# A transformer block on one core: a new order of jobs in the up-projection, and VectorE's small operations of differential attention as steps of their own

## The chip, the cores and the metric
The kernel runs on one core of one Trainium2 chip. The metric is device time in microseconds, the median of 3 runs. "Faster" and "slower" are against the kernel before.

## The reference, cut to what matters
One block over 2048 tokens and 16 meta tokens in front of them, float32 throughout. Two groups of heads run on the same input. The first is differential attention with ALiBi:

```
s1 = q1 k1^T * scale + bias ;  s2 = q2 k2^T * scale + bias      (per head, 4 heads)
a  = softmax(s1) - lam * softmax(s2) ;  o = a v
```

The second is latent attention (4 heads), whose queries are `_rms(cq) @ w_q_up` with a rotary part. Both outputs go through `w_o`, an RMSNorm and the residual; a squared-ReLU MLP of width 4096 follows. The mask lets a query see the chunks of 64 keys up to its own, so row tile i of 128 queries reads 16 + 128 (i + 1) keys.

## The kernel before, in words
The stages run one after the other: projections, `up-projection` of the latent queries, differential attention, latent attention, output product, MLP. A stage is a program for each engine, written in order; the engines meet only through semaphores that count up. Where an operation needs float32 accuracy from PE's fast format, an operand is split: ScalarE rounds it to a high half, VectorE subtracts to get the low half, and PE adds three products.

**Up-projection (line 797).** A list `jobs` (lines 838 to 840) sets the order on all engines at once. A job is a `turn` (four transposes of a weight), a `fold` (query weights times key weights), a `rope` half (rotary queries of a piece of 512 tokens), a `q` (the other queries of a head) or a `vo` (values' weights times w_o). PE writes the job's sums into the next of 8 banks and waits until the job 8 banks back has been taken. `takers` gives who takes them: VectorE rotates ropes (two multiplications each, GpSimd adds them), and copies of `q` and `vo` go to ScalarE and VectorE in turn. Results go to one of 8 output slots, `slot(engine, i)`: the slot is free once the store that used it 8 results before has landed. SP issues the stores in the order of the jobs, and at the first half of rope pieces 2 and 3 loads for the next stage in front of them. At the same two places, `WO_AT` (line 840), ScalarE makes the high half of a part of w_o (2 of 4 heads), VectorE the low half, and the `vo` products behind it wait for that (`wo_lo_ready`). At the second of them ScalarE first loads the table for exponentials.

**Differential attention (from line 1167).** For each of 4 heads, row tiles i = 0 to 15 with two components c. A row is cut in chunks of at most 512 keys (`row_chunks`). For a chunk PE makes scores in one of 4 banks; VectorE adds the bias, writes the row and keeps a maximum (L1535, a second instruction reads the accumulator); behind a row's last chunk it reduces the maxima to minus the row's maximum (L1542). ScalarE takes the exponential over the whole row with its sum (L1481). For component 0 VectorE takes the reciprocal of the sum (L1567) and GpSimd scales the row (L1473). For component 1 VectorE takes the reciprocal (L1574), multiplies by minus lambda (L1576), and adds both components (L1580): "the sum of row tile i" below. When the four row tiles of a group are summed, PE transposes them tile by tile (L1646), ScalarE copies (L1494) and PE multiplies by the values (L1660).

`head_steps` writes one order of steps for all engines: `chunk`, `exp`, `scale`, `end`, and between them `turn`, `product` and `out`, spread over three phases of a head (row tiles 0 to 7, 8 to 11, 12 to 15) by a cost of each step of VectorE. The first phase holds the turns of the last group of the head before, the second those of groups 0 and 1, the third those of group 2. The first turn of a group isn't put in front of its last `end`. `SCALE_AFTER` and `END_AFTER` say how many chunks later a row's scaling and sum come. Each engine walks the same list and does the steps that are its own.

## Time and profile before
| | us |
|---|---|
| median of 3 runs | 2596.75 (2596.61 to 2596.9) |
| profiled execution | 2593.93, its span 2592.2 |
| up-projection | about 391.9 to 426.6 |
| differential attention | about 426.6 to 796 |
| PE busy, share of the span | 2531.8, 98% |
| VectorE | 1613.4, 62% |
| ScalarE | 1212.7, 47% |
| GpSimd | 333.4, 13% |

Times in the rows are microseconds from the span's start. A busy engine can still be late: "idle before" names what ended the time in which it had nothing to run, and a matmul's duration is its latency, while the next one starts before it ends.

### The profile page before, as it was taken

What the parts mean: (1) busy time and instruction counts of PE and PEld (TensorE: products, weight loads), DVE (VectorE), ACT (ScalarE), POOL (GpSimd) and SP (SyncE); (2) the same over time, 40 slices, a digit from 0 to 9 for tenths busy, and PEclk for the clock granted to TensorE, in tenths of its full rate; (3) what the DMA queues carried; (4) which work ended last, traced back from release to release, by engine and by line L of the source; (5) the groups of instructions that cost most, each with busy time, mean ns of one, the idle gap of its engine ahead of it and who ended that gap; (6) DMA issues with size and microseconds to landing.
All of it is one profiled execution on the core that took longest, in us unless ns stands there. A gap on an engine that the chain in (4) does not pass through costs nothing.

```text
span 2592.2 us, 35303 instructions
## 1 busy us (share of the span) xinstructions
PE 2531.8 (98%) x12172; PEld 2107.2 (81%) x12172; DVE 1613.4 (62%) x3499; ACT 1212.7 (47%) x2183; POOL 333.4 (13%) x368
## 2 busy tenths in 40 slices
PE   8999999999999999989999999999999999999997
PEld 8998887676667999978877888888888888888886
DVE  6123307998985776654468777867758465564765
ACT  6112314777765555554544333533335353443544
POOL 2110002222211222210000000000000001121143
PEclk9999999999999999999999999999999999999999
DMA  7334458554342111145677666666655365776787
GB/s 236 119 106 125 123 163 261 136 135 99 82 140 85 34 29 46 42 130 161 194 240 223 210 219 215 219 193 209 190 163 175 118 216 106 179 161 164 200 162 136
DMA packets 328892, 398.33 MB, mean 154 GB/s; under 512 B 20864, under 2 KB 235120, under 8 KB 320400
## 3 DMA queue, kind: packets, MB, share of 16 engines
q1 hardware_dynamic: 311152, 364.15, 44.6%
q0 software_dynamic: 17568, 31.99, 8.5%
q8 instruction: 95, 1.56, 0.2%
q14 instruction: 77, 0.63, 0.1%
HBM read 239.60 MB, written 156.48 MB: 153 GB/s over the span
## 4 chain that ended last, share of the span: by engine, by line
PE 62%; DVE 3%; DMA 1%; ACT 1%; issue 1%; SPq 0%; POOL 0%; DVEq 0%; ACTq 0%; POOLq 0%
PE ff_ps_x L3266 26%; PE ff_ps_m L3266 13%; PE ff_ps_z L3266 6%; PE ml_ps_s L2143 6%; PE ff_ps_m L1699 4%; PE ml_ps_o L2172 4%; PE ml_ps_t L2156 2%; DMA ml_v_raw<-scr_yT 1%; DMA ff_pieces<-scr_acc 0%; PE ff_ps_r L2703 0%; PE mo_ps_t L2720 0%; SPq L2330 0%; DVE ff_pieces L2433 0%; DVE ff_pieces L2624 0%; DVE ff_pieces L2620 0%
## 5 line engine op out<-in xcount | busy, mean ns | idle before, releaser
L3266 PE MATMUL ff_ps_x<-ff_mv_hi_p,ff_st_hi_p 128*128 128x512 f32 x764 | 297.8, 390 | 0.5 <-ACT ff_u L3006 0.5
L3266 PE MATMUL ff_ps_x<-ff_mv_hi_p,ff_st_lo_p 128*128 128x512 f32 x764 | 297.3, 389 | 0.0
L3266 PE MATMUL ff_ps_x<-ff_mv_lo_p,ff_st_hi_p 128*128 128x512 f32 x764 | 297.2, 389 | 0.0
L2143 PE MATMUL ml_ps_s<-wide,ml_qs 128*128 128x416 f32 (+14 forms) x880 | 194.4, 353 | 4.1 <-PEq L137 2.8
L3112 DVE TENSOR_TENSOR ff_st_lo_p<-ff_ps_m,ff_st_hi_p 128x512 fp32r<-128x512 f32 x190 | 130.5, 687 | 103.4 <-ACT ff_st_hi_p L2989 103.4
L2956 POOL DMA_DIRECT2D scr_acc<-ff_pieces x64 | 55.6, 874 | 1015.2 <-DVE ff_pieces L3136 946.7
L3006 ACT ACTIVATE ff_u<-ff_ps_x 128x512 f32<-128x512 f32 x128 | 76.6, 598 | 214.8 <-PE ff_ps_x L3266 214.8
L3266 PEld LDWEIGHTS ff_ps_x<-ff_mv_hi_p,ff_st_hi_p 128*128 128x128 f32 x764 | 143.4, 188 | 32.5 <-issue 2.0
L3266 PEld LDWEIGHTS ff_ps_x<-ff_mv_hi_p,ff_st_lo_p 128*128 128x128 f32 x764 | 143.4, 188 | 30.0
L3266 PEld LDWEIGHTS ff_ps_x<-ff_mv_lo_p,ff_st_hi_p 128*128 128x128 f32 x764 | 143.4, 188 | 29.5
L2143 PEld LDWEIGHTS ml_ps_s<-wide,ml_qs 128*128 128x128 f32 x880 | 150.4, 188 | 17.0 <-issue 2.9
L2989 ACT ACTIVATE ff_st_hi_p<-st_raw 128x512 fp32r<-128x512 f32 x191 | 119.4, 626 | 86.2 <-PE ff_ps_z L3266 86.2
L3266 PE MATMUL ff_ps_m<-wide,ff_st_hi_p 128*128 128x512 f32 x512 | 157.7, 389 | 0.4 <-DVE ff_st_lo_p L2607 0.4
L2989 ACT ACTIVATE ff_st_hi_p<-ff_ps_m 128x512 fp32r<-128x512 f32 x190 | 113.2, 598 | 93.6 <-PE ff_ps_m L3266 93.6
L3266 PE MATMUL ff_ps_x<-wide,ff_st_hi_p 128*128 128x512 f32 x504 | 155.1, 389 | 0.0
L3112 DVE TENSOR_TENSOR ff_st_lo_p<-st_raw,ff_st_hi_p 128x512 fp32r<-128x512 f32 x191 | 130.8, 687 | 36.9 <-ACT ff_st_hi_p L2989 35.6
L2058 DVE CUSTOM_DVE_ANT_0 ml_rows<-ml_ps_s,ahead_bias 128x416 f32<-128x416 f32 (+14 forms) x176 | 100.1, 570 | 70.4 <-PE ml_ps_s L2143 62.6
L1660 PE MATMUL da_ps_o<-da_pT,da_v 128*128 128x512 f32 (+3 forms) x320 | 137.2, 529 | 0.0
L1981 ACT ACTIVATE ml_pT_hi<-ml_ps_t 128x512 fp32r<-128x512 f32 (+3 forms) x176 | 90.8, 538 | 93.3 <-PE ml_ps_t L2156 92.9
L2080 DVE TENSOR_TENSOR ml_pT_lo<-ml_ps_t,ml_pT_hi 128x512 fp32r<-128x512 f32 (+3 forms) x176 | 105.2, 615 | 41.6 <-ACT ml_pT_hi L1981 41.3
L1613 PE MATMUL da_ps_s<-da_keys,ahead_q 128*128 128x416 f32 (+14 forms) x352 | 112.5, 423 | 2.4 <-DVE da_mx L1535 2.4
L3266 PEld LDWEIGHTS ff_ps_m<-wide,ff_st_hi_p 128*128 128x128 f32 x512 | 96.0, 188 | 20.5 <-issue 0.6
(318 smaller groups left out, 6329.4 us busy)
## 6 DMA issues: line engine op xcount, KB each, us to landing
st_raw<-in_w_ff SPq DMA_DIRECT2D x64, 512.0 KB, 6.4
scr_hid<-ff_pieces SPq DMA_DIRECT2D x128, 256.0 KB, 2.7
st_raw<-scr_hid SPq DMA_DIRECT2D x64, 512.0 KB, 5.3
ring<-in_w_ff SPq DMA_DIRECT2D x28, 1024.0 KB, 7.5
scr_t<-ring SPq DMA_DIRECT2D x24, 1024.0 KB, 5.6
ring<-scr_t SPq DMA_DIRECT2D x21, 1024.0 KB, 7.6
scr_acc<-ff_pieces POOLq DMA_DIRECT2D x64, 256.0 KB, 4.0
ring<-scr_u SPq DMA_DIRECT2D x13, 1024.0 KB, 8.0
```

The costliest lines, as they stand in the source:

```text
L1613: m = pe.matmul(ps_s[n % NSB][:, 0:w], qs[:, g % 2, c, P * b:P * b + P], keys[u][:, 2 * c + j, k0:k0 + w], start=j == 0, stop=j == 1)
L1660: pe.matmul(ps_o[:, c0:512], v_meta[:, :] if t == 0 else v[:, t - 1], pT[0:rows_of, n % NPT, c0:512], start=t == 0, stop=t == tiles_of(g) ...
L1699: m = pe.matmul(bank, y[a][:, k], w[b][:, cols], start=k == 0 and i == 0, stop=k == KD - 1 and i == 2, skip_group_check=True)
L1981: act.activation(pT_hi[0:rows_of, n % NPT, c0:512], ps_t[n % NTB][0:rows_of, c0:512], ACT.Copy).then_inc(hi_copied, 1)
L2058: dve.tensor_tensor_reduce(out=row(i, u)[:, k0:k0 + w], in0=ps_s[n % NSB][:, 0:w], in1=bias[:, b0:b0 + w], scale=1.0, scalar=LOWEST, op0=A ...
L2080: dve.tensor_tensor(pT_lo[0:rows_of, n % NPT, c0:512], ps_t[n % NTB][0:rows_of, c0:512], f32(pT_hi[0:rows_of, n % NPT, c0:512]), ALU.subtr ...
L2143: m = pe.matmul(ps_s[n % NSB][:, 0:w], q, k, start=j == 0, stop=j == len(pairs) - 1)
L2172: m = pe.matmul(ps_o[:, c0:512], v[0:rows_of, at_v], p, start=t == 0 and j == 0, stop=t == tiles_of(g) - 1 and j == 2)
L2989: act.activation(st_hi[kind][:, :, :], stationary(kind, n % 2), ACT.Copy).then_inc(st_hi_ready, 1)
L3006: act.activation(tile, bank[:, :], ACT.Copy).then_inc(taken, 1)
L3112: dve.tensor_tensor(st_lo[kind][:, :, :], stationary(kind, n % 2), f32(st_hi[kind][:, :, :]), ALU.subtract).then_inc(st_lo_ready, 1)
L3266: m = pe.matmul(bank[:, :], w[kind][:, k], a[kind][:, k], start=start and k == 0 and i == 0, stop=stop and k == KH - 1 and i == 2, skip_gr ...
```

## The change
In the up-projection the list of jobs has a new order. In differential attention the small operations of VectorE become steps of their own, a chunk or more behind what they read: `most` (the row's maximum), `invert` and `weigh` (the two in front of the sum). A row's sum comes a few chunks after its second component ends, counted by the next row's chunks, and in front of its successor's scaling. The small tiles have four slots in place of two; the second components of row tiles 0 to 2 lie beside one another. A cost in the planner goes from 250 to 100.

```
-        jobs += [("q", 0, h) for h in range(MLA_H)] + [("turn", TURN_V)] + ropes_of(2) + folds_of((0, 1)) + ropes_of(3) + folds_of((2, 3))
+        jobs += ropes_of(2) + [("turn", TURN_V)] + [("q", 0, h) for h in range(2)] + folds_of((0, 1))
+        jobs += [("q", 0, h) for h in range(2, MLA_H)] + ropes_of(3) + folds_of((2, 3))
...
         def comp_row(i, c, u):
-            return row(i, u) if c == 0 else second[:, i % 2, 0:META + P * (i + 1)]
+            if c == 0:
+                return row(i, u)
+            start, wide = (sum(META + P * (a + 1) for a in range(i)), 0) if i < 3 else (0, i % 2)
+            return second[:, wide, start:start + META + P * (i + 1)]
...
-                        steps += [step for _, step in later if step[2] - NT * step[1] < i]
-                        later = [(left, step) for left, step in later if step[2] - NT * step[1] >= i]
-                        later.append((1, ("exp", 0, i, c)))
+                        due = i if c == COMPS - 1 else i - 1
+                        if i < 3:
+                            due = -1
+                        steps += [step for _, step in later if step[2] - NT * step[1] < due]
+                        later = [(left, step) for left, step in later if step[2] - NT * step[1] >= due]
+                        later += [(1, ("most", 0, i, c)), (1, ("exp", 0, i, c))]
                         if c == 0:
                             later.append((SCALE_AFTER, ("scale", 0, i)))
                         if c == COMPS - 1:
-                            later.append((END_AFTER, ("end", 0, i)))
+                            later += [(after, (kind, 0, i)) for kind, after in zip(("invert", "weigh", "end"), end_after(i))]
...
+        def end_after(i):
+            first = {NT - 1: 5, 0: 3, 1: 3, 2: 3}.get(i) or len(row_chunks(i + 1)) + 1
+            return first, first + 1, first + 2
...
-            return META + P * (step[2] + 1) + 250 if step[0] == "end" else 0
+            return META + P * (step[2] + 1) + 100 if step[0] == "end" else 0
...
-        SCALE_AFTER, END_AFTER = 2, 5
+        SCALE_AFTER = 3
...
+                if c == 1 and k0 == 0 and not (first_head and i < 4):
+                    dve.wait_ge(probs_ready, NT * h + (-1 if i < 3 else 0 if i == 3 else i - 1))
...
-                if k0 + w == META + P * (i + 1):
-                    dve.wait_ge(scores_read, NCH * h + n + 1)
-                    dve.tensor_scalar(nmax_all[:, 0:nth + 1], mx[:, i % 2, c, 0:nth + 1], -scale, None, ALU.mult, ALU.min,
-                                      accum_out=nmax[:, i % 2, c:c + 1]).then_inc(max_ready, 1)
...
+            def most(h, i, c, **at):
+                last = max(n for n, chunk in enumerate(chunks) if chunk[:2] == (i, c))
+                parts = len(row_chunks(i))
+                dve.wait_ge(scores_read, NCH * h + last + 1)
+                dve.tensor_scalar(mx[:, i % 4, c, 0:parts], mx[:, i % 4, c, 0:parts], -scale, None, ALU.mult, ALU.min,
+                                  accum_out=nmax[:, i % 4, c:c + 1]).then_inc(max_ready, 1)
...
-            heads(dve, {"chunk": chunk, "scale": invert, "end": end})
+            heads(dve, {"chunk": chunk, "most": most, "scale": invert_first, "invert": invert_second, "weigh": weigh_second, "end": end})
```

`invert_first`, `invert_second` and `weigh_second` hold the three small operations of before, each behind its own wait; `end` keeps the addition.

## Rows read from the trace of the kernel before
**Rows 1.** Stretches: length; busy of PE, PEld, DVE, ACT, POOL; PE clock, DMA, GB/s
```profile
402.40:426.60 24.20, 18.94 (x78) 14.88 (x77) 15.87 (x20) 9.19 (x10) 7.75 (x7) 0.93 1.04 323
426.60:454.00 27.40, 27.05 (x135) 23.16 (x134) 24.62 (x124) 18.74 (x44) 5.84 (x8) 1.00 0.76 240
454.00:512.30 58.30, 54.85 (x270) 40.26 (x269) 55.00 (x194) 42.24 (x65) 13.28 (x9) 1.00 0.65 150
512.30:598.80 86.50, 83.50 (x417) 61.43 (x417) 78.46 (x305) 63.17 (x112) 19.08 (x16) 1.00 0.45 111
```
**Rows 2.** Timeline, end of head 1: start, us, engine, line, operation [idle <-releaser]
```profile
591.51 0.63 PE L1613 MATMUL da_ps_s<-da_keys,ahead_q 128*128 128x400 f32 x2 [0.75 <-DVE da_mx L1535]
592.37 3.43 PE L1660 MATMUL da_ps_o<-da_pT,da_v 128*128 128x512 f32 x8
598.79 1.09 PE L1646 MATMUL da_ps_t<-ident,da_rows 128*128 128x128 f32 x8 [1.25 <-DVE da_rows L1580]
...
593.78 2.02 ACT L1481 ACTIVATE da_second<-da_second,da_nmax 128x2064 f32<-128x2064 f32 x1 [2.64 <-DVE da_nmax_all L1542]
...
595.92 0.17 DVE L1574 RECIPROCAL da_inv<-da_total 128x1 f32<-128x1 f32 x1 [1.61 <-ACT da_second L1481]
```
**Rows 3.** Timeline of PE, for the pace of scores and of transposes
```profile
585.79 1.09 PE L1613 MATMUL da_ps_s<-da_keys,ahead_q 128*128 128x416 f32 x5
...
642.54 0.60 PE L1646 MATMUL da_ps_t<-ident,da_rows 128*128 128x128 f32 x4
```
**Rows 4.** Timeline of PE in the up-projection
```profile
413.35 0.47 PE L989 MATMUL mu_ps<-mu_wo_hi,mu_turned_hi 128*128 128x512 f32 x1 [2.15 <-DVE mu_wo_lo L962]
...
422.18 0.47 PE L989 MATMUL mu_ps<-mu_wo_hi,mu_turned_hi 128*128 128x512 f32 x1 [3.12 <-DVE mu_wo_lo L962]
...
424.09 0.63 PE L989 MATMUL mu_ps<-mu_wo_hi,mu_turned_hi 128*128 128x512 f32 x1
```
**Rows 5.** Timeline of the up-projection on VectorE, GpSimd and ScalarE
```profile
402.64 2.48 DVE L975 TENSOR_TENSOR mu_rot<-mu_ps,up_trig 128x512 f32<-128x512 f32 x4 [1.42 <-issue]
410.91 2.29 DVE L962 TENSOR_TENSOR mu_wo_lo<-mu_wo_first,mu_wo_hi 128x2048 fp32r<-128x2048 f32 x1 [1.11 <-ACT mu_wo_hi L946]
...
404.01 2.55 POOL L933 TENSOR_TENSOR mu_out<-mu_rot 128x512 f32<-128x512 f32 x2 [2.54 <-DVE mu_rot L975]
...
415.89 0.60 ACT L953 ACTIVATE mu_out<-mu_ps 128x512 f32<-128x512 f32 x1 [0.92 <-DMA scr_mq<-mu_out]
```
**Rows 6.** DMA issues (last: us to landing); below, the eight stores until 410.9
```profile
scr_w_vo<-mu_out SPq DMA_DIRECT2D x8, 256.0 KB, 4.9
mu_wo_first<-in_w_o SPq DMA_DIRECT2D x1, 1024.0 KB, 5.0
...
L925 SPq DMA_DIRECT2D scr_mq<-mu_out x4: 467/1071/1327, 407.0 to 410.0; - x4
DMA to landing us min/median/max: 7.6/8.3/10.6
```
**Rows 7.** Timeline of VectorE in head 2, row tiles 11 to 13
```profile
655.88 0.16 DVE L1567 RECIPROCAL da_inv<-da_total 128x1 f32<-128x1 f32 x1
655.95 0.60 DVE L1535 CUSTOM_DVE_ANT_0 da_second<-da_ps_s,ahead_bias 128x448 f32<-128x448 f32 x1
...
656.91 0.09 DVE L1535 DVE_READ_ACCUMULATOR2_ANT da_mx<- 128x1 f32 x1
657.03 0.16 DVE L1542 TENSOR_SCALAR_CACHE_REDUCE da_nmax_all<-da_mx 128x4 f32<-128x4 f32 x1
...
657.15 0.66 DVE L1535 CUSTOM_DVE_ANT_0 da_rows<-da_ps_s,ahead_bias 128x480 f32<-128x480 f32 x1
...
659.55 0.16 DVE L1574 RECIPROCAL da_inv<-da_total 128x1 f32<-128x1 f32 x1
659.74 0.21 DVE L1576 TENSOR_SCALAR da_inv<-da_inv,da_lam 128x1 f32<-128x1 f32 x1
659.99 1.97 DVE L1580 SCALAR_TENSOR_TENSOR da_rows<-da_second,da_inv,da_rows 128x1680 f32<-128x1680 f32 x1
```

More of the change, by code:

```diff
@@ L1559, in minus_lambda, with invert_first @@
                 dve.wait_ge(lam_step, 4)
-            def invert(h, i, u, **at):
+            def invert_first(h, i, u, **at):
                 dve.wait_ge(exp_ready, NT * COMPS * h + COMPS * i + 1)
-                if not (isinstance(h, int) and h == 0 and i < 2):
-                    dve.wait_ge(first_scaled, NT * h + i - 1)
-                dve.reciprocal(inv[:, i % 2, 0:1], total[:, i % 2, 0:1]).then_inc(inv_ready, 1)
-            def end(h, i, u, **at):
+                if not (isinstance(h, int) and h == 0 and i < 4):
+                    dve.wait_ge(first_scaled, NT * h + i - 3)
+                dve.reciprocal(inv[:, i % 4, 0:1], total[:, i % 4, 0:1]).then_inc(inv_ready, 1)
@@ L1575, in end @@
-                dve.wait_ge(inv2_step, n + 1)
-                dve.tensor_scalar(inv2[:, i % 2:i % 2 + 1], inv[:, i % 2, 1:2], lam[:, 3:4], None, ALU.mult).then_inc(inv2_step, 1)
-                dve.wait_ge(inv2_step, n + 2)
+                dve.wait_ge(second_inverted, NT * h + i + 1)
+                dve.tensor_scalar(inv2[:, i % 4:i % 4 + 1], inv[:, i % 4, 1:2], lam[:, 3:4], None, ALU.mult).then_inc(second_weighed, 1)
+            def end(h, i, u, **at):
+                dve.wait_ge(second_weighed, NT * h + i + 1)
@@ L1578, in end @@
                 dve.wait_ge(first_scaled, NT * h + i + 1)
-                dve.scalar_tensor_tensor(out=row(i, u), in0=comp_row(i, 1, u), scalar=inv2[:, i % 2:i % 2 + 1], in1=row(i, u),
+                dve.scalar_tensor_tensor(out=row(i, u), in0=comp_row(i, 1, u), scalar=inv2[:, i % 4:i % 4 + 1], in1=row(i, u),
                                          op0=ALU.mult, op1=ALU.add).then_inc(probs_ready, 1)
-            heads(dve, {"chunk": chunk, "scale": invert, "end": end})
+            heads(dve, {"chunk": chunk, "most": most, "scale": invert_first, "invert": invert_second, "weigh": weigh_second, "end": end})
```

28 lines of the change are left out of this document (14 added, 14 removed).

## The prediction
> **What bounds the kernel now.** I read the page first: PE is busy 98% of the span and VectorE 62%, but the change touches only 390 to 796 us, so the share of the span says little. The table of stretches [rows 1] is the next thing: from 402.4 to 426.6 us (the up-projection after its first jobs) PE is busy 18.9 of 24.2 us at a mean granted clock of 0.93; in differential attention PE and VectorE are both nearly full, 83.5 and 78.5 of 86.5 us for each head in the middle. A head lasts 86.5 us: the stretches are cut where PE waits for the sum of row tile 15 [rows 1, 2].
>
> Which of the two it is that ends a wait in attention, the waits of PE show: 0.75 us behind VectorE's reads at the end of a head, 1.25 us for the sum of row tile 15 (the first transposes of the last group) [rows 2]. Read from start to start, where one matmul should follow the other at its own pace, these and the small ones come to about 4.3 us a head. The rest, about 82 us, is PE's own work. I check that: 8 product matmuls take 3.43 us from first start to last end, so 0.43 us each; 4 transposes take 0.60 us with 0.27 us of that the last one's, so 0.11 each; score matmuls of 416 columns come every 0.185 us (5 in 1.09 us, the last one 0.35) [rows 2, 3]. A head has 88 product matmuls with 38,912 columns (32.6 us), 152 transposes (16.7 us) and 176 score matmuls with 70,656 columns (31.4 us): 80.7 us, and a little for the changes between kinds. So VectorE can save at most 4.3 us a head before PE is the bound.
>
> **Part 1, the new order of jobs.** In the order of before PE waits twice for the low half of w_o, 2.15 and 3.12 us. Soon behind the second wait a matmul takes 0.63 us in place of 0.47 [rows 4]: the granted clock is at the lower level, 1.2 in place of 2.4 GHz, after those 3.1 us without work. A mean of 0.93 over 24.2 us [rows 1] makes that 1.7 us lost. Behind the first wait of 2.15 us the matmuls stay short.
>
> First wait, after: PE starts rope piece 2 at 402.4 us, in place of the queries, and has 12 matmuls of 512 columns for it (0.23 us each at the score rate of [rows 3], 2.7 us), 0.4 us for the turn of v and 2.7 for two queries: it is at its first fold at 408.2 us. VectorE's queue in front of that fold: rotations of piece 1 from 402.64 us (2.48), low half of w_o (2.29), rotations of piece 2 (2.48), low half of the turned v (the size of a rotation's quarter, 0.7 us) [rows 5]. That is 410.6 us, so PE waits 2.4 us. The first part of w_o landed 5.0 us after its issue [rows 6], before any of this, so nothing waits for it. Two queries (2.7 us) are then still to do, which were done at 413.35 us before: the two orders are level. No gain.
>
> Second wait, after: PE is through with rope piece 3 at 418.9 us, as before. What it waits for is a chain: ScalarE's copy of query 2, load of its table, high half of w_o, VectorE's low half. Before, the copy in front of the table load began at 415.89 us, itself released by a store that had landed [rows 5], and PE went on at 422.18: 6.29 us from copy to PE. In the new order the sums of query 2 are there at 414.9 us; if the copy began then, PE would go on 1 us earlier, and might keep its clock: 1.0 + 1.7 = 2.7 us gained. But query 2 now has output slot 4 (of 8, the 13th store), which rope (2,0) has used, and must wait until that has landed. VectorE rotates piece 2 only from 407.4 us; GpSimd's addition starts 1.37 us after a rotation starts (402.64 to 404.01) and takes 1.28, so the store is issued at 410.1 us. By then SP has issued as many bytes as before (three 256 KB query stores then, 0.78 MB of queries and bias now, which its place in front of rope piece 2 brings forward), and the store issued at 410.0 us landed after 7.6 us [rows 6]. So the copy starts at 417.6 us in place of 415.89: +1.7 us. The ends of this cost: -2.7 us (lands at once; the later stores of the folds took 4.9 us in the median, which would be -0.9) and +4.5 us (the slowest store's 10.6 us) [rows 6]. I take +1.7; the lower clock is lost either way. VectorE's copy of query 3 waits for the next slot until 418.6 us, in the cover of ScalarE's table load and high half. On SP the keys of the third group are issued behind the same four folds as before, near 420 us, and are read only near 454 us.
>
> What follows is PE-bound until 454 us (27.05 of 27.4 us [rows 1]), so the 1.7 us reach the end.
>
> **Part 2, what VectorE saves.** A small operation that depends on the one before it: the accumulator's read starts at 656.91 us, the reduction behind it at 657.03, its own read at 657.11, the next read of scores at 657.15: 0.24 us. One that depends on nothing recent: read of the accumulator and reciprocal both at 655.88, the next scores at 655.95, 0.07 us [rows 7]. So each of 128 maxima gains 0.16 us behind the next chunk (0.12 of wait, 0.04 of start). Of the pair in front of a sum, reciprocal 659.55, product 659.74, sum 659.99: 0.44 us, of which two independent steps would leave 0.08 + 0.12 (the product's 0.21 is longer than the reciprocal's 0.16): 0.24 gained for each of 64 sums. Together 20 + 15 = 35 us of VectorE's time over four heads, 9 a head. To it comes the wait for ScalarE's last exponential of a head, 1.61 us [rows 2], under which now lie reads of the next head. The new wait in front of the second component's first chunk asks for a sum two row tiles back: nothing. Between no gain of VectorE at all (the durations of [rows 7] in any place) and 35 us I take 35; the row of the reciprocal is the same kind of operation in the same place.
>
> The Trainium skill speaks against this. "VectorE: DVE Perf Modes", in the section "The DRAIN you can't avoid", says that the next operation starts only when the pipeline is empty, that the semaphore costs nothing, and advises to save operations, not waits. By that rule the 35 us would be near 0, and the result that of the last rival below; these rows do not agree, since the held reduction starts 0.12 us later than the free reciprocal does.
>
> **Part 3, what becomes of it.** VectorE's 9 us a head are more than PE's 4.3 us of waits, so PE decides, and its waits for sums move. I wrote out both orders of steps.
> - Row tile 11's sum, which PE needs for the first transpose of the third group, came right behind the first component of row tile 12, three chunks of scores before that transpose in every head. Now it stands behind the third of four chunks of the second component, and PE's queue has only the last two, narrow products of the group before (256 and 128 columns twice, 0.65 us) between that chunk and the transpose. VectorE needs 0.54 for the chunk (448 columns at 1.04 ns and 0.08 to start, the pace of the sums) and 1.83 for the sum (the 1.97 of row tile 12's, less 128 columns) [rows 7]: PE waits 2.37 - 0.65 = 1.7 us, in all four heads. New.
> - Row tile 15's sum: from the start of the head's last chunk VectorE has, at that pace, 0.49 for it, 0.23 for the next head's first, 0.16 until the maximum is there; from the start of ScalarE's exponential to the reciprocal are 2.14 us (593.78 to 595.92); in its cover the next four chunks; then the reciprocal, one more chunk (0.5), small steps (0.4), another chunk (0.38), the sum (1.97 and three times 128 columns, 2.37, less 0.08 of overlap): 7.0 us. PE has 5.8 us of work from there to its transpose (six products 3.9, seven chunks 1.9) and is 0.7 us ahead, because VectorE has just done row tile 14's sum: 2.0 us of wait, where 0.75 + 1.25 us and a wait for ScalarE's first copy stand now [rows 2].
> - What goes besides these: the small waits for reads.
> So a head in the middle has about 3.8 us of waits in place of 4.3: 0.5 us gained, 1.5 over three. In head 0, which has no products of a head before it, VectorE is the bound from 454 us on (55.0 of 58.3 us busy [rows 1]): there 8 row tiles give 0.56 us each, 4.5 us, less 1.7 of the new wait and what PE allows: 2.3 us. The tail behind the last scores is as long as before, since no chunk is left to lie in front. Scaling by GpSimd, busy 19 of 86.5 us, starts a chunk later and in front of nothing that waits.
>
> **The sum.** +1.7 - 1.5 - 2.3 = -2.1 us. Against the profiled execution (span 2592.2, with what lies around it 2593.93 us) that is 2591.8; against the median, 2.8 us higher, 2594.6.
>
> **Rivals.** A measurement of this kernel tells 0.2% (5.2 us) from no change.
> - *PE's waits mostly go.* If VectorE's lead is large enough at both sums, only one wait of 1.3 us a head is left of 4.3: 3 us gained a head, 12 in all, 2586.5 with part 1. For it: 9 us of VectorE's time a head. Against it: at the sum of row tile 11 PE's queue is empty by the order itself, whatever VectorE's lead.
> - *The store lands in time.* Part 1 gains 2.7 in place of losing 1.7: 2590.2. For it: fewer small stores in front. Against it: none of the eight issued before 411 us landed within 7.5 us [rows 6].
> - *Slower: VectorE is behind at the two sums.* Each chunk that it lags there (0.54 us) is added to PE's wait, at 4 + 3 places: 3.8 us a chunk. PE can be up to 4 chunks ahead, the number of score banks. From two chunks of lag on it is slower than before (2602), at three 2606. For it: between the two sums VectorE has some 22 us of work in PE's 21. Against it: PE has just held more work than VectorE in front of row tile 11's sum.
> - *The small operations cost as much between reads as behind them.* Then VectorE saves nothing, the stretch from row tile 11's sum to that of 15 takes 31.3 in place of 29 us, a head 0.8 us more than now: 2600.5.
>
> **How the numbers follow.** Forecast 45% (its own range 2591 to 2598.5), waits go 22%, store in time 12%, VectorE behind 13%, no saving 8%. The range reaches into the first and the slower rival: 2586 to 2603. Faster by over 0.2%: 22 + 10 + 5 = 37%; slower 11 + 3 + 1 = 15%; same 48%.
>
> **What would show it.** PE waiting some 1.7 us for the sum at the first transpose of the third group in each head, and some 2 us at row tile 15's, with no wait for reads at a head's end beyond 0.3 us; maxima and reciprocals on VectorE with no idle time in front; heads of 86 us; in the up-projection ScalarE's copy of query 2 released by a store, and a second wait of PE near 5 us. The prediction is wrong if a head is under 84.5 or over 87.5 us, or if that copy starts before 416 us.

## The result and the profile after

The changed kernel takes 2612.42 us in the median (2611.51 to 2612.98), the kernel before 2596.72 us beside it: the ratio is 1.0064, 95% interval 1.0052 to 1.0076. Forecast were 2594.6 us in a range to 2603. The change makes the kernel slower, and both halves of it do (the experiments below).

The profiled executions differ by 19.0 us of span (2611.2 against 2592.2). By the starts of the stages and heads in the two timelines that is: attention starts 3.4 us later, head 0 is 0.5 us longer, heads 1 and 2 are 5.1 and 4.8 us longer (91.4 us each), the last head with the tail 4.0, and 1.3 us come later. By the prediction's own sign (a head over 87.5 us) it is wrong.

First the stretches that answer to [rows 1], of after (columns as there); the third and fourth are cut, as before, where PE waits for row tile 15's sum.

```profile
402.40:430.00 27.60, 20.25 (x80) 15.92 (x79) 15.94 (x20) 7.59 (x10) 9.80 (x7) 0.89 0.99 315
430.00:457.40 27.40, 27.40 (x137) 23.82 (x135) 22.00 (x121) 18.22 (x44) 5.12 (x7) 0.99 0.65 202
457.40:518.90 61.50, 54.70 (x271) 40.92 (x270) 56.16 (x220) 44.99 (x74) 14.98 (x11) 1.00 0.61 147
518.90:610.40 91.50, 85.84 (x417) 64.52 (x417) 75.09 (x305) 63.53 (x112) 19.21 (x16) 0.96 0.43 105
```

VectorE is busy 75.1 us where it was 78.5, so its work did get less. PE is busy 85.8 where it was 83.5, with the same 417 matmuls, at a clock of 0.96 where it was 1.00: its work didn't grow, it was done more slowly. And PE is idle 5.7 us of the head where it was idle 3.0.

The up-projection, timeline of after on PE, ScalarE and VectorE (start, us, engine, line, operation, idle before and its releaser), against [rows 4, 5]:

```profile
411.17 0.47 PE L990 MATMUL mu_ps<-mu_wo_hi,mu_turned_hi 128*128 128x512 f32 x1 [2.24 <-DVE mu_turned_lo L967]
...
424.71 0.77 PE L990 MATMUL mu_ps<-mu_wo_hi,mu_turned_hi 128*128 128x512 f32 x1 [5.11 <-DVE mu_wo_lo L963]
...
418.41 0.60 ACT L954 ACTIVATE mu_out<-mu_ps 128x512 f32<-128x512 f32 x1 [2.71 <-DMA scr_mqr<-mu_out]
419.03 1.28 ACT L945 ACT_TABLE_LOAD   x1
420.32 1.91 ACT L947 ACTIVATE mu_wo_hi<-mu_wo_second 128x2048 fp32r<-128x2048 f32 x1
...
419.50 0.69 DVE L982 COPY mu_out<-mu_ps 128x512 f32<-128x512 f32 x1 [3.48 <-DMA scr_mqr<-mu_out]
422.27 2.29 DVE L963 TENSOR_TENSOR mu_wo_lo<-mu_wo_second,mu_wo_hi 128x2048 fp32r<-128x2048 f32 x1 [2.08 <-ACT mu_wo_hi L947]
```

PE waits 2.24 and 5.11 us, where it waited 2.15 and 3.12. The second wait is the chain forecast: a copy of a query waits for a store, behind it in ScalarE's queue stand the table load and the high half of w_o, and VectorE's low half ends the wait. The first matmul behind it takes 0.77 us, so the clock is down. The stretch at the lower clock (after) is:

```profile
424.00:430.80 6.80, 6.09 (x17) 4.96 (x17) 4.17 (x7) 1.19 (x2) 2.66 (x3) 0.50 0.93 271
```

PE is busy for 6.1 of its 6.8 us, the first 0.7 us still belong to the wait. So it costs 3.0 us, where the 3.4 us of the kernel before cost 1.7.

VectorE's small operations, timeline of after, against [rows 7]:

```profile
687.06 0.08 DVE L1549 DVE_READ_ACCUMULATOR2_ANT da_mx<- 128x1 f32 x1
687.06 0.15 DVE L1561 TENSOR_SCALAR_CACHE_REDUCE da_mx<-da_mx 128x4 f32<-128x4 f32 x1
687.14 0.08 DVE L1561 DVE_READ_ACCUMULATOR da_mx<-da_mx 128x1 f32 x1
687.14 0.59 DVE L1549 CUSTOM_DVE_ANT_0 da_rows<-da_ps_s,ahead_bias 128x416 f32<-128x416 f32 x1
...
690.33 0.21 DVE L1594 TENSOR_SCALAR da_inv<-da_inv,da_lam 128x1 f32<-128x1 f32 x1
690.45 0.58 DVE L1549 CUSTOM_DVE_ANT_0 da_second<-da_ps_s,ahead_bias 128x416 f32<-128x416 f32 x1
```

The reduction starts with the accumulator's read and the next scores start 0.08 us later; the product costs 0.12. In the kernel before the same reduction kept VectorE for 0.24 us. At this place the forecast holds to the hundredth. Its total doesn't show: 9 us of VectorE's time a head were forecast, its busy time fell by 3.4, and all of its gaps under 0.15 us came to no more than 2.3 us a head before.

PE in the same head, timeline of after, around its three waits:

```profile
610.37 1.59 PE L1666 MATMUL da_ps_t<-ident,da_rows 128*128 128x128 f32 x12 [2.34 <-DVE da_rows L1600]
...
614.38 0.96 PE L1666 MATMUL da_ps_t<-ident,da_rows 128*128 128x128 f32 x4
...
668.56 0.66 PE L1666 MATMUL da_ps_t<-ident,da_rows 128*128 128x128 f32 x4 [1.93 <-DVE da_rows L1600]
...
672.31 1.01 PE L1666 MATMUL da_ps_t<-ident,da_rows 128*128 128x128 f32 x4
...
693.81 0.52 PE L1633 MATMUL da_ps_s<-da_keys,ahead_q 128*128 128x272 f32 x2 [1.10 <-DVE da_mx L1549]
```

PE waits 2.34 us for row tile 15's sum (1.25 in [rows 2]), 1.93 for row tile 11's (a new wait), and at the head's end it still waits 1.10 for reads. And a group of 4 transposes takes 0.96 and 1.01 us behind the first two waits, where [rows 3] has 0.60. The same head cut at the clock (stretches of after; the clock is third from the end):

```profile
602.75:611.70 8.95, 6.61 (x35) 4.67 (x33) 6.74 (x39) 5.81 (x15) 2.12 (x3) 1.00 0.30 83
611.70:615.10 3.40, 3.40 (x13) 2.35 (x11) 1.47 (x8) 1.59 (x5) 0.77 (x1) 0.50 0.02 5
615.10:669.70 54.60, 52.43 (x264) 39.17 (x263) 44.67 (x185) 38.43 (x70) 11.16 (x10) 1.00 0.61 146
669.70:673.10 3.40, 3.40 (x15) 2.88 (x13) 2.34 (x9) 2.30 (x4) 0.72 (x1) 0.50 0.91 218
673.10:694.20 21.10, 20.00 (x103) 15.29 (x102) 20.07 (x71) 15.24 (x23) 4.45 (x3) 1.00 0.03 4
```

Two stretches of 3.4 us at 1.2 GHz, each just behind a wait, and each with PE busy throughout. Read in this way over the whole of attention, after has six such stretches, before has one, in the tail:

```profile
771.20:774.60 3.40, 2.90 (x13) 2.90 (x14) 3.27 (x7) 1.20 (x2) 0.00 (x0) 0.51 0.00 0
```

Of after's seven new or longer waits for sums, idle 1.93 us (row tile 11) and 2.34 us (row tile 15), five have such a stretch behind them: head 0's at row tile 11 and head 2's at row tile 15 have none. The sixth stretch is in the tail, behind 3.33 us. A PE that is full does half as much in 3.4 us, so one stretch costs 1.7 us.

### The profile page after: what moved, and what is told of

The parts are those of the page before. It is cut to its first block, busy times and chain, and to the rows that moved or that the text cites. A ratio compares the mean times of both kernels' runs of the same rounds, so it can differ in the third digit from the quotient of the medians.

```text
span 2611.2 us, 35301 instructions
## 1 busy us (share of the span) xinstructions
PE 2537.2 (97%) x12172; PEld 2116.0 (81%) x12172; DVE 1599.0 (61%) x3499; ACT 1212.5 (46%) x2183; POOL 335.8 (13%) x368
## 4 chain that ended last, share of the span: by engine, by line
PE 62%; DVE 3%; DMA 1%; ACT 1%; issue 1%; SPq 0%; POOL 0%; DVEq 0%; ACTq 0%; POOLq 0%
PE ff_ps_x L3286 26%; PE ff_ps_m L3286 13%; PE ff_ps_z L3286 6%; PE ml_ps_s L2163 6%; PE ff_ps_m L1719 4%; PE ml_ps_o L2192 4%; PE ml_ps_t L2176 2%; DMA ml_v_raw<-scr_yT 1%; DMA ff_pieces<-scr_acc 0%; PE ff_ps_r L2723 0%; PE mo_ps_t L2740 0%; SPq L2350 0%; DVE ff_pieces L2453 0%; DVE ff_pieces L2644 0%; DVE ff_pieces L2640 0%
## 5 line engine op out<-in xcount | busy, mean ns | idle before, releaser
L2001 ACT ACTIVATE ml_pT_hi<-ml_ps_t 128x512 fp32r<-128x512 f32 (+3 forms) x176 | 90.7, 538 | 93.4 <-PE ml_ps_t L2176 91.6
L1666 PE MATMUL da_ps_t<-ident,da_rows 128*128 128x128 f32 x608 | 96.9, 283 | 18.1 <-DVE da_rows L1600 18.1
```

Source lines behind the costliest of these rows:

```text
L1666: m = pe.transpose(ps_t[n % NTB][0:rows_of, P * b:P * b + P], row(4 * g + b, u)[:, k0:k0 + rows_of], ident[:, :])
L2001: act.activation(pT_hi[0:rows_of, n % NPT, c0:512], ps_t[n % NTB][0:rows_of, c0:512], ACT.Copy).then_inc(hi_copied, 1)
```

## The experiments

All times are medians; "ratio" is against the kernel before, run on the same chip beside them.

**Each half alone.** The kernel before with the new order of jobs, and the changed kernel with the old order:

```
-        jobs += [("q", 0, h) for h in range(MLA_H)] + [("turn", TURN_V)] + ropes_of(2) + folds_of((0, 1)) + ropes_of(3) + folds_of((2, 3))
+        jobs += ropes_of(2) + [("turn", TURN_V)] + [("q", 0, h) for h in range(2)] + folds_of((0, 1))
+        jobs += [("q", 0, h) for h in range(2, MLA_H)] + ropes_of(3) + folds_of((2, 3))
```

> The kernel before with the new order of jobs alone. Theory: after's trace has PE wait 5.11 us at its second wait for the low half of w_o in place of 3.12, since ScalarE's copy of query 2 stood 2.71 us until a store of a rope had landed, and the granted clock is at the lower level for 6.8 us from 423.9 us on in place of 3.4; differential attention begins 3.4 us later in after, and that is what this order costs: 2600 us, heads of attention at 86.5 us. Rival: the order costs nothing by itself, and the start is late for another reason (the stage before it ended 0.45 us later): 2597.

> The changed kernel with the old order of jobs. Theory: the rest of the loss lies in attention, where after's heads last 91.4 us in place of 86.5 and PE waits 2.1 us for row tile 11's sum and 2.5 us for row tile 15's; 2596.7 + 12 to 14 = 2609 to 2611 us. Rival: a good part of attention's loss comes from its late start and the loads that collide with it, then heads are shorter here than 91 us and the time is under 2606.

Measured: the order alone 2600.46 us against 2596.65, ratio 1.0013 (1.0003 to 1.0022); the steps alone 2607.76, ratio 1.0043 (1.0028 to 1.0058). The order alone is where its expectation had it, the steps alone 1.2 us below theirs. The two losses together, some 0.56%, are the whole change's 0.64% within their intervals: two faults that add up, the larger in attention.

**The sums sooner.** If PE waits because the sums come two chunks later, put them back to the chunk they had:

```
-            first = {NT - 1: 5, 0: 3, 1: 3, 2: 3}.get(i) or len(row_chunks(i + 1)) + 1
-            return first, first + 1, first + 2
+            return (5, 5, 5) if i == NT - 1 else (3, 4, 5)
```

> As the one before (old jobs, small operations as steps), but a row's two small operations and its sum come 3, 4 and 5 chunks behind its second component in every row (5, 5, 5 for row tile 15), so that row tile 11's sum is again one chunk into the second component of row tile 12. Theory (the place of the sums, and not the separate small operations, makes PE wait, and each wait of over 2 us has a stretch at the lower clock behind it, 1.7 us): no wait at the first transpose of the third group, about 1.3 us at row tile 15's, no lower clock between 450 and 760 us, heads of 84 us: 2586 to 2591 us. Rival (the separate small operations themselves delay ScalarE's exponentials and PE): heads stay above 88 us, 2603 or more.

Measured 2627.32 us, ratio 1.0119 (1.0102 to 1.0136): a miss, 20 us slower than the steps alone. Timeline of this kernel, VectorE and ScalarE at row tiles 12 and 13:

```profile
677.25 1.96 DVE L1598 SCALAR_TENSOR_TENSOR da_rows<-da_second,da_inv,da_rows 128x1680 f32<-128x1680 f32 x1
679.13 0.15 DVE L1559 TENSOR_SCALAR_CACHE_REDUCE da_mx<-da_mx 128x4 f32<-128x4 f32 x1
...
679.33 1.81 ACT L1490 ACTIVATE da_rows<-da_rows,da_nmax 128x1808 f32<-128x1808 f32 x1 [2.42 <-DVE da_mx L1559]
...
681.25 0.16 DVE L1582 RECIPROCAL da_inv<-da_total 128x1 f32<-128x1 f32 x1 [0.81 <-ACT da_rows L1490]
```

The maximum is a step one chunk behind its row, and that is the chunk at which the earlier sum falls. The sum, 1.96 us, stands in front of it; the exponential starts that much later (ScalarE waited 2.42 us for the maximum); and two chunks on VectorE itself stands idle 0.81 us for the exponential's total. Moved as steps, the maximum and the sum compete for one place. The changed kernel avoids this by its later sums: that is what their lateness is for, and its price is PE's waits.

**The maximum alone as a step.** Reciprocal, product and sum of the second component together 5 chunks behind the row, the first reciprocal 2 chunks behind, as before the change (the planner's cost and the rule for overdue steps are those of before, too; they aren't shown below):

```
+            return 5, 5, 5
...
+        SCALE_AFTER = 2
```

> Old jobs; of the small operations only the reduction of the maxima is a step of its own, a chunk behind; reciprocal, product and sum stand together 5 chunks behind the row as before, with the planner's old cost and the old rule for what is flushed. Theory: VectorE gains 0.16 us for each of 128 maxima, the waits for sums stay as before, 1.3 us at row tile 15's: heads of 85 us, 2591 to 2594 us. Rival (a later maximum delays the exponential, and with it the copies that PE needs): 2598 or more.

Measured 2663.1 us, ratio 1.0255 (1.0238 to 1.0273), against 2591 to 2594 expected: the worst of all. Waits in one head of this kernel (us in total, times, longest):

```profile
ACT da_rows L1488 <- DVE da_mx L1557: 27.3, 16, 3.2
DVE da_inv L1580 <- ACT da_rows L1488: 14.2, 16, 1.7
DVE da_inv L1584 <- ACT da_second L1488: 8.2, 14, 2.2
```

The same view of the kernel before has 1.2 us, once, in place of the first row, and 0.8 and 1.6 us, once each, in place of the others. Maximum, exponential, reciprocal is a ring between two engines that wait in order. With a chunk added in front of the exponential and none in front of the reciprocal, VectorE waits once for every row, and each wait delays the next maximum. How much of the 66 us this ring costs isn't shown: a sum stands ahead of a maximum here as in sums_early (the sum starts at 658.27, the maximum behind it at 659.79), and attention has some 41 us at the lower clock, up to 20 us of the loss. Neither was tried apart.

**What PE's waits and the clock are worth.** Two edits on the steps alone. One puts both groups' transposes later in the list, the other leaves them and gives PE something to do in the wait (the wait for the bank that the unread transposes write moves in front of them, which isn't shown below):

```
-        PHASES = (((0, 1), ((1, 3),), 0.2, 7), ((2,), ((0, 0), (0, 1)), 0.15, 7), ((3,), ((0, 2),), 0.2, 7))
+        PHASES = (((0, 1), ((1, 3),), 0.4, 7), ((2,), ((0, 0), (0, 1)), 0.15, 7), ((3,), ((0, 2),), 0.3, 7))
...
+                    if g >= 2:
+                        for k in range(12):
+                            pe.transpose(ps_t[n % NTB][:, 0:P], ident[:, :], ident[:, :])
                     pe.wait_ge(probs_ready, NT * h + 4 * g + 4)
```

> Differential attention as in the changed kernel, the old order of jobs in the up-projection, and the transposes of the last group (after row tile 15's sum) and of the third group (after row tile 11's sum) placed about four chunks of scores later in the list. The kernel with the same steps and the transposes at their old places took 2607.8 us. Theory A (the whole loss of attention is TensorE waiting at these two places for a sum that now comes two chunks later, 2.5 + 2.1 us a head, and its lower clock behind the wait, 1.7 us each): both waits fall under 0.5 us, the clock stays up, the heads go back to about 86.5 us from 91.4, and the time is 2590 to 2598 us. Theory B (VectorE's order itself costs it, the exponential and the second sum's place among the reads): waits of the same size come up elsewhere, heads stay at 90 to 91 us, 2604 to 2610 us.

> Differential attention as in the changed kernel, the old order of jobs; ahead of the wait for row tile 11's and for row tile 15's sum TensorE makes 12 transposes of the identity that nobody reads, so that it works through most of a wait that is there anyway. Without them the kernel took 2607.8 us. Theory A (a good half of the loss is the granted clock, which falls behind these waits): the low stretches in attention go away, 6 of them by 1.7 us is 10 us, and the time is 2597 to 2601 us with the waits themselves nearly unchanged in total. Theory B (the clock follows something else, or the time at the lower clock is hidden by VectorE's work): 2606 to 2610 us. If the 12 transposes are longer than the waits, each head becomes up to 0.5 us longer.

Later transposes: 2601.38 us, ratio 1.0029 (1.0019 to 1.004). Kept busy: 2600.79, ratio 1.0024 (1.0014 to 1.0033). By the ratios they win back 3.6 and 5 of the 11 us; the first lies between the ranges of its two theories. PE at the last group's first transpose, first in the kernel kept busy, then in the one with later transposes (timelines):

```profile
603.74 0.71 PE L1662 MATMUL da_ps_t<-ident 128*128 128x128 f32 x5
605.49 1.53 PE L1668 MATMUL da_ps_t<-ident,da_rows 128*128 128x128 f32 x12 [1.03 <-DVE da_rows L1599]
```

```profile
602.45 0.54 PE L1632 MATMUL da_ps_s<-wide,ahead_q 128*128 128x304 f32 x2 [1.73 <-DVE da_mx L1548]
607.16 1.13 PE L1679 MATMUL da_ps_o<-da_pT,da_v_meta 128*128 128x512 f32 x2 [1.92 <-ACT da_pT L1504]
```

With the unread transposes PE still arrives at the sum too early (1.03 us idle instead of 2.34), no sum comes sooner, and yet heads 1 and 2 are 88.2 and 88.3 us instead of 89.8 and 91.6: the granted clock is 1.00 from 429 to 779 us, where the steps alone have three low stretches, one in head 1 and two in head 2. That is what the clock alone cost there. Moving the last group's transposes removes its wait, but in the place of one wait of 2.3 us come two, for VectorE's reads (1.73) and for ScalarE's copies (1.92): turns pushed into a shorter stretch meet their copies late. Theory B was right for this group. (The clock stayed up behind these waits, in all three heads.)

**The maximum in front of the early sum**, and **the second reciprocal and its product alone**, in two versions (the three edits in this order; the last version also has the second reciprocal 3 instead of 2 chunks behind, and the planner's cost back at 250):

```
-                    steps += [step for left, step in later if left <= 0]
+                    steps += sorted((step for left, step in later if left <= 0), key=lambda step: step[0] not in ("most", "exp"))
...
                         steps += [step for _, step in later if step[2] - NT * step[1] < due]
                         later = [(left, step) for left, step in later if step[2] - NT * step[1] >= due]
+                        steps.append(("most", 0, i, c))
...
                     steps += [("chunk", 0, n)]
+                    if k0 + w == META + P * (i + 1):
+                        steps.append(("most", 0, i, c))
```

> Differential attention as in the changed kernel with the old order of jobs, but the sum early (5 chunks behind its row, as before the change) and, where a row's maximum and another row's sum fall on the same chunk, the maximum in front. With the sum in front of the maximum the same places took 2627.3 us. Theory A (that loss was the exponential, which started a sum of 2 us late): the waits of ScalarE for the maximum and of VectorE for the exponential's total go away, transposes of row tiles 11 and 15 don't wait over 1 us, and the time is 2590 to 2600 us. Theory B (the maximum a chunk later is too late whatever stands around it): VectorE still waits for ScalarE, 2610 to 2625 us.

> The kernel before with one part of the change: the second reciprocal and its product with lambda as steps of their own ahead of the sum (2 and 3 chunks behind the row), four slots of the small tiles; the maximum right behind its last read, exponential, first reciprocal, scaling and sum at the places of before. Theory A (VectorE's small operations are worth time where nothing is displaced): VectorE saves 0.1 to 0.24 us at each of 64 sums, 7 to 15 us of its work; what PE waits for sums at the transposes and heads' ends (some 2 us a head before) becomes less: 2590 to 2595 us. Theory B (VectorE has idle time in the heads anyway): no change, 2596 to 2597.5 us. In neither is it slower than 2600 us unless the second reciprocal comes before the exponential is done.

> The kernel before with one part of the change: second reciprocal and its product as steps of their own, where they fit ahead of the sum (3 and 4 chunks behind the row); maximum right behind its last read and ahead of any sum, and all other steps at the places of before. The version of it in which the maximum came behind a sum of another row took 2638 us. Theory A (that loss was the maximum standing behind a sum of 2 us, so that the exponential and then VectorE itself started late): ScalarE's waits for the maximum are back at 11 to 12 us in 90, heads at 86 to 87 us, 2592 to 2598 us. Theory B (VectorE's waits for the exponential's total, 7.7 + 7.7 us in a head, come from the new small steps themselves): heads stay over 89 us, 2605 to 2640 us. On the worth of the small operations: if VectorE's work bounds the head, some 0.1 us at 30 sums is 3 us less in attention; if not, no change against 2596.

With the maximum in front, the early sums take 2612.52 us, ratio 1.007 (1.0053 to 1.0087): 0.49% less, 13 us, than with the sum in front, and still 0.27% more than with the change's own places. The two kernels differ in nothing but this order. ScalarE's wait for the maximum of first components falls from 17.1 to 10.2 us in a head, VectorE's waits for a total from 8.6 to 4.8: the time lies in theory B's range, though theory A's waits did become shorter. The version called max_at_once was meant to have the maximum of before, but where a sum is overdue at its row's end it put it behind that sum: 2638.25 us, ratio 1.017 (1.0153 to 1.0187). The expectation hadn't seen this order; what it did name as a way to more than 2600 us, a second reciprocal ahead of its exponential, is there too (VectorE waited 7.7 us a head at it). As second_split, with the order mended, the second reciprocal a chunk later and the old cost, it takes 2599.69 us, ratio 1.0012 (1.0002 to 1.0022), 1.7 us above theory A's range (one of its ten executions took 5636 us, which nothing here explains). Which of the three differences makes those 39 us wasn't tried apart. And the second reciprocal as a step wins nothing here: a head is 87.2 to 87.4 us, VectorE waits 2.5 us for ScalarE at it, and PE waits more than before at the head's end.

**The third group's transposes alone.** On the steps alone, in three kernels and a control on the kernel before: the start of the third phase from 0.2 to 0.3, with and without the unread transposes in the last group's wait, and the sum 6 chunks behind its row (there the first phase starts at 0.3 too).

> Differential attention as in the changed kernel, the old order of jobs, the transposes of the third group (after row tile 11's sum) four chunks of scores later in the list, and 12 transposes of the identity that nobody reads ahead of the wait for row tile 15's sum alone. Moving both groups' transposes gave heads of 88.3 us, where the scores of the small rows waited 1.9 us for VectorE and a product 2.1 us for ScalarE in place of the wait for row tile 15; filling both waits gave 88.3 us too. Theory A (each of the two waits is worth its own length, and moving the third group costs nothing elsewhere): heads of 86.5 to 87.3 us, 2595 to 2599 us. Theory B (VectorE, 85 us of work in a head with what it waits for, is the bound by now, and TensorE's waits only show it): heads stay at 88.2 us, 2600 to 2602 us.

> Differential attention as in the changed kernel with the old order of jobs, but the sum one chunk earlier (6 behind its row) and everywhere behind the maximum of the row after it, and the transposes of the third group one chunk or two later in the list. Theory A (the changed kernel's loss is the two waits for late sums and the clock behind them): both waits fall from 2.5 and 2.1 us to under 1.5, too short for the clock to fall, heads of 87 us, 2595 to 2600 us. Theory B (sooner sums cost as much in ScalarE's exponential as they win at the transposes, as where they stood 5 chunks behind): heads of 89 to 91 us, 2603 to 2612 us.

> Differential attention as in the changed kernel, the old order of jobs, the third group's transposes four chunks later, nothing made in the wait for row tile 15's sum. Theory A (that wait of 2.5 us is followed by the lower clock, 1.7 us a head in up to three heads): heads of 87.5 to 88 us against 86.05 with the wait filled, one low stretch after each such wait, 2596 to 2599 us. Theory B (the filling transposes did nothing by themselves): heads of 86.1 us, 2592 to 2594 us.

> The kernel before with the third group's transposes placed some four chunks of scores later and nothing else. It had a wait of 0.75 us ahead of a score and of 1.4 us for row tile 15's sum in a head, and none over 0.6 us at the third group. Theory A (the mended version wins by VectorE's small operations, and the place of these transposes is only a mend): 2595 to 2598 us, no change from the kernel before. Theory B (the place itself is worth it): 2592 to 2594 us.

Third group later and the other wait filled: 2592.38 us, ratio 0.9989 (0.998 to 0.9999), heads of 86.05 us, better than theory A's 2595 to 2599. Unfilled: 2597.72, ratio 1.0005 (0.9995 to 1.0015). The sum one chunk sooner: 2601.79, ratio 1.0019 (1.001 to 1.0029), heads of 88.3 us, between its theories' ranges: the loss turned into many small waits and one of 1.43 us at the head's end, behind which the clock fell in two heads. The kernel before with the third group later: 2597.29, ratio 1.0004 (0.9994 to 1.0013), so the place of those transposes is worth nothing by itself. What third_later wins over it is 0.15%, 4 us by the ratios. Without the 12 unread transposes nothing of this is left (1.0005 against 1.0004), since the longer wait for row tile 15's sum brings the lower clock. Where the clock stays up, VectorE's small operations as steps win some 0.45 us a head (86.05 and 86.08 against 86.52). What the unread transposes would have won in the kernel before wasn't tried.

The unfilled kernel shows the price of the clock inside one run. Its heads 1 and 2 (stretches), and PE at the same wait in each (timeline):

```profile
506.81:592.89 86.08, 82.81 (x419) 61.88 (x417) 74.54 (x307) 62.89 (x112) 19.25 (x17) 1.00 0.45 111
592.89:680.63 87.74, 84.46 (x418) 63.00 (x417) 74.88 (x305) 63.07 (x112) 19.29 (x17) 0.98 0.45 109
```

```profile
514.43 1.53 PE L1665 MATMUL da_ps_t<-ident,da_rows 128*128 128x128 f32 x12 [2.34 <-DVE da_rows L1599]
516.02 1.02 PE L1679 MATMUL da_ps_o<-da_pT,da_v_meta 128*128 128x512 f32 x2
...
600.51 2.16 PE L1665 MATMUL da_ps_t<-ident,da_rows 128*128 128x128 f32 x12 [2.34 <-DVE da_rows L1599]
602.89 1.92 PE L1679 MATMUL da_ps_o<-da_pT,da_v_meta 128*128 128x512 f32 x2
```

The same wait of 2.34 us stands in both heads. Behind the second the clock falls and the head is 1.66 us longer; behind the first it doesn't, and the head is as short as with the wait filled. So within one run and with the same wait the clock alone makes 1.7 us.

**The up-projection mended.** The second half of w_o ahead of the copies that wait for slots, on the kernel with the new order alone:

```
-        WO_AT = {jobs.index(("rope", piece, 0)): piece - 2 for piece in (2, 3)}
+        WO_AT = {jobs.index(("rope", 2, 0)): 0, jobs.index(("q", 0, 2)): 1}
```

> The kernel before with the new order of jobs in the up-projection, and the load of ScalarE's table, the rounding of the second half of w_o and VectorE's subtraction of it made ahead of the copies of queries 2 and 3 instead of behind them. With the new order alone the time was 2600.5 us, and TensorE waited 6.4 us for VectorE's subtraction, which stood behind copies that waited for the stores of the position parts out of their slots. Theory A (that queue behind the slots' stores is the whole of the second wait): the subtraction ends near 419 us, TensorE's second wait falls under 1.5 us, attention starts 5 us sooner than with the order alone, and with the lower clock behind that wait gone too the time is 2593 to 2596 us. Theory B (the second half of w_o itself, or the copies, come late anyway): the wait goes over to a copy's bank or to the loading of w_o, and at most 2 us are won: 2598 to 2601 us.

Measured 2590.83 us, ratio 0.9984 (0.9974 to 0.9993), better than theory A's 2593 to 2596. Timeline of this kernel, VectorE and PE:

```profile
418.33 2.29 DVE L963 TENSOR_TENSOR mu_wo_lo<-mu_wo_second,mu_wo_hi 128x2048 fp32r<-128x2048 f32 x1 [2.59 <-ACT mu_wo_hi L947]
...
420.77 0.47 PE L990 MATMUL mu_ps<-mu_wo_hi,mu_turned_hi 128*128 128x512 f32 x1 [1.39 <-DVE mu_wo_lo L963]
```

PE waits 1.39 us where the order alone made it wait 6.40, and the matmul behind it takes 0.47 us: no lower clock. The stores land hardly sooner (ScalarE's copy that waits for one starts at 419.1 us, 419.4 with the order alone); nothing that PE needs stands behind it any more. Attention starts at 423.7 us, against 430.7 with the order alone and 426.6 before.

**Both mended together.**

> The changed kernel in full with the faults found so far mended: the second half of w_o rounded and subtracted ahead of the copies of queries 2 and 3 (worth 2600.5 to 2590.8 us with the new order alone), the third group's transposes four chunks later and 12 unread transposes ahead of the wait for row tile 15's sum (2607.8 to 2592.4 us with the old order). Theory A (the two halves are independent): the gains over the kernel before add up, 5.6 + 4.1 us off 2596.4, so 2586 to 2588 us. Theory B (an earlier start of attention only meets loads that aren't there yet, or the clock falls elsewhere): 2589 to 2593 us.

Measured 2589.18 us against 2595.6, ratio 0.9978 (0.9968 to 0.9987). The product of the two single ratios is 0.9973, so the addition of theory A stands within the intervals, though the median missed its 2586 to 2588 by 1.2 us and lies in theory B's range. What B gave as reasons doesn't show: no stretch at the lower clock from 380 to 830 us, and heads as in third_later. This version beats both kernels, the changed one by 0.86% and the one before by 0.13 to 0.32%. Its heads 1 and 2:

```profile
502.90:588.96 86.06, 84.11 (x430) 63.15 (x429) 74.28 (x305) 62.84 (x112) 19.18 (x17) 1.00 0.46 111
588.96:675.03 86.07, 84.12 (x430) 63.16 (x429) 74.83 (x305) 62.81 (x112) 19.19 (x17) 1.00 0.47 111
```

## Why the prediction was wrong, step by step

The step that failed is in Part 3: a head in the middle was to have 3.8 us of PE's waits in place of 4.3, each priced at its own length, with nothing for the clock behind it. Measured, PE's idle time rose from 3.0 to 5.7 us a head, and two stretches at the lower clock took 3.4 us more. The steps one by one:

- *Up-projection, waits.* The places were right, and so were the causes: 2.4 us forecast and 2.24 measured for the first wait, near 5 and 5.11 for the second. The store of rope (2,0) landed 6.5 us after its issue instead of 7.6, but it was issued at 411.85 instead of 410.1, behind three loads that SP issued from 409.44 to 411.80. So the copy started at 418.4, not 417.6, and PE went on at 424.7, not 423.9: 2.5 us later than before, where 1.7 were forecast.
- *Up-projection, the clock: failed.* "The lower clock is lost either way" took one stretch of it for both orders. Behind 5.1 us of wait it lasted 6.8 us instead of 3.4. 0.7 us of that lay in the wait, so it cost another 1.3 us, 0.8 of them ahead of attention's start and 0.4 behind it. Hence attention started 3.4 us late (2.5 + 0.8) and not 1.7. The order alone measured 3.8 us, and with the second wait at 1.39 us instead of 6.40 it took 5.6 us less than the kernel before.
- *VectorE's small operations.* Right one by one: 0.08 us for a reduction or a reciprocal and 0.12 for the product, where a reduction stood at 0.24 and the pair at 0.44. Too large as a total: of 9 us a head the rows show 3.4 in busy time and can hide at most 2.3 in gaps. Since PE decides, this isn't what made the time wrong. The rule of the Trainium skill that spoke against it ("VectorE: DVE Perf Modes", section "The DRAIN you can't avoid": the semaphore costs nothing) is not borne out for operations this small. A remark in the same section, that a next operation which isn't held starts earlier, fits these rows: the reduction without a wait in front starts with the accumulator's read, and the next scores 0.08 us later. (The advice to save operations stands under "Rules for kernel authors" on that page, not in the section that the prediction names.)
- *The two new waits for sums.* Right in place, too small in size: 1.7 and 2.0 us forecast, 2.1 and 2.5 us from the start that the pace allows (idle 1.93 and 2.34 in the rows). Together 0.9 us a head.
- *"No wait for reads at a head's end beyond 0.3 us": failed.* It is 1.10 us. VectorE has row tile 14's sum there two chunks later than before, so that its savings arrive behind it.
- *"What goes besides these: the small waits". Failed, and by the largest term.* A wait was priced at its own length, and the clock in attention at nothing, without a reason given. Behind the new waits (idle 1.93 and 2.34 us) and in the tail PE's clock has low stretches, five more in attention than before, 8.5 us of the 14.4 that attention lost. [Rows 4] had shown a fall behind 3.12 us and none behind 2.15; one wait without a fall didn't make waits of that length free of it. That the clock is the cause and not a companion, kept_busy and third_unfilled show: about 1.7 us for each stretch that goes, and the sums no sooner.
- *Head 0, 2.3 us gained: failed.* It lost 0.5. In it are waits of 1.93 us for row tile 11's sum (1.7 forecast) and of 1.10 us for reads at its end (none forecast), and no stretch at the lower clock. What else took the gain wasn't tried. With the third group's transposes moved (third_later) it gains 1.7 us: 79.2 us from its first scores to head 1, against 80.9.
- *The rival "VectorE is behind at the two sums"* gave 2602 to 2606 us for more lag. It named the place, and the sum of the change's steps alone (2607.8) is near it, but not its mechanism: half of the loss is the clock, and the waits for the two sums were hardly longer than the forecast's.
- *The range.* The result lies 9.4 us above it. Its upper end, 2603, had one bound for attention and one for the store, and none for the clock, though PE's clock was an unknown at every new wait of about 2 us. Seven such waits by 1.7 us are 12 us on the slow side; five of the seven cost it.

So of the 19 us in the profile about 10 are the clock (five stretches more in attention, 8.5 us, and 1.3 in the up-projection), and the rest is waits: 2 us in the up-projection, the new wait for row tile 11's sum (2.1 us in four heads) and the longer one for row tile 15's (1.1 us in each head with a next one), less what VectorE's savings gave. What makes the last head and its tail 4.0 us longer wasn't tried by itself; two of the low stretches lie in it, against one before, which is 1.7 us. Nor is it known where the last 1.3 us, behind attention, come from.

## What to carry to other kernels

In these runs a wait of PE of about 2 us cost up to nearly its double: give every new one a chance of the lower clock behind it, or give the engine some unread work in it. When small operations are moved out of an engine's way, write down which long operation they now stand behind: here a maximum behind a 2 us sum instead of ahead of it cost 13 us. And look for what can be mended before giving a change up: with w_o's second half sooner, one group's transposes later and one wait filled, 0.64% slower became 0.22% faster. Where a copy waits for an output slot, look at what is queued behind the copy before looking for more slots.

## What the runs showed of the hardware

- PE's clock fell to 1.2 GHz for 3.4 us behind many waits of 1.9 to 2.3 us in attention, and not behind every one: behind five of the changed kernel's seven (outside the tail), behind three of seven with the steps alone, behind one of three in third_unfilled, where the same 2.34 us wait did it at 600.5 us and not at 514.4, and behind none of later_turns' six of 1.7 to 1.9 us. The up-projection's first wait of 2.2 us was followed by a low stretch in some of the kernels (kept_busy, 414.7 us) and not in others. In the kernel before it never fell behind the 1.25 us at the heads' ends. Shorter waits were no guarantee: behind 1.4 us with other waits close to it, it fell in sum_after_six (509.9 and 598.7 us) and in max_first (508.8 and 601.0 us). Behind 5.1 to 6.4 us it was low for 6.8 us.
- Twelve transposes of the identity, about 1.3 us of work (0.71 us for 5 in the row above, the last one's latency in it), in a wait of 2.34 us left 1.03 us of idle time and kept the clock up each time: three times each in kept_busy, third_later and both_mended. In kept_busy's tail 2.02 us of the wait were left, and the clock fell at 779.9 us.
- A reciprocal or a reduction of VectorE to one element a partition occupies it for 0.07 to 0.08 us when nothing holds it, the product with a scalar 0.12.
